# Modulation chunks moved out of the setup stage of a two-block transformer kernel, and semaphores cleared by range

## The reference, cut to what matters

```
c_act = silu(c)
for l in range(2):
    mod = c_act @ w_ada[l] + b_ada[l]              # w_ada[l]: 1024 x 6144
    shift1, scale1, gate1, shift2, scale2, gate2 = split(mod, 6)
    h = rms_norm(x, norm1_g[l]) * (1 + scale1) + shift1
    x = x + gate1 * mix(h)                         # attention and convolution
    h2 = rms_norm(x, norm2_g[l]) * (1 + scale2) + shift2
    x = x + gate2 * expert_choice_ffn(h2, ...)     # router, softmax, top_k, experts
```

## Time and profile before

| | us |
|---|---|
| median of the runs shown (3) | 3978.43 |
| their range | 3977.78 to 3983.3 |
| the profiled execution | 3975.68 |
| its span | 3973.9 |

### The profile page before, as it was taken

One profiled execution on the slowest core, in us unless ns is written; L12 is line 12 of the kernel. 1 busy time (PEld: TensorE's weight loads), 2 busy tenths in 40 slices (PEclk: granted clock), 3 DMA queues, 4 the chain that ended last, 5 costly groups with the idle time before them and its releaser, 6 DMA issues. The chain is left out here.

```text
span 3973.9 us, 47220 instructions
## 1 busy us (share of the span) xinstructions
PE 3517.1 (89%) x16392; PEld 2800.9 (70%) x16392; DVE 2466.7 (62%) x2229; ACT 1648.8 (41%) x1644; POOL 1170.1 (29%) x688
## 2 busy tenths in 40 slices
PE   4798798779999969879949999969998789999998
PEld 1375597558888757378728888857877678888886
DVE  7787775478888769777358888865118431212124
ACT  5521443258888630244227888843115110000101
POOL 0142233311111124133321111104542535453632
PEclk9899899889999979989969999989998889999999
DMA  9610001469999720000049999952100211111111
GB/s 339 242 38 18 10 14 38 164 242 395 395 395 396 299 77 32 14 15 20 32 186 358 394 393 395 394 203 95 48 29 0 85 38 58 53 42 53 43 52 53
DMA packets 143147, 610.67 MB, mean 154 GB/s; under 512 B 16480, under 2 KB 34272, under 8 KB 93920
## 3 DMA queue, kind: packets, MB, share of 16 engines
q1 hardware_dynamic: 133856, 576.21, 37.7%
q0 software_dynamic: 9216, 33.56, 3.3%
HBM read 563.06 MB, written 41.94 MB: 152 GB/s over the span
## 5 line engine op out<-in xcount | busy, mean ns | idle before, releaser
L1630 DVE TENSOR_TENSOR ex_lo<-ex_raw,ex_hi 128x2048 fp32r<-128x2048 f32 x378 | 858.5, 2291 | 115.6 <-ACT ex_hi L1580 115.0
L1580 ACT CAST ex_hi<-ex_raw 128x2048 fp32r<-128x2048 f32 x378 | 720.7, 1914 | 139.6 <-PE psum L1542 139.6
L1540 PE MATMUL psum<-ex_hi,xe_hi 128*128 128x512 f32 x1024 | 404.1, 395 | 1.3 <-DVE xe_lo L1635 1.3
L1542 PE MATMUL psum<-ex_hi,xe_lo 128*128 128x512 f32 x1024 | 400.7, 391 | 0.0
L1541 PE MATMUL psum<-ex_lo,xe_hi 128*128 128x512 f32 x1024 | 400.3, 391 | 0.0
L516 DVE SCALAR_TENSOR_TENSOR mix<-y,lcols,mix 128x1024 f32<-128x1024 f32 x176 | 278.8, 1585 | 5.7
L2399 DVE TENSOR_TENSOR ff_full<-psum,ff_full 128x1024 f32<-128x1024 f32 x22 | 26.9, 1225 | 408.4 <-PE psum L431 408.4
L416 POOL TENSOR_SCALAR up_hi<-up_raw 128x1024 fp32r<-128x1024 f32 x44 | 122.1, 2776 | 361.6 <-PE psum L431 337.6
L431 PE MATMUL psum<-hn_hi,up_hi 128*128 128x512 f32 x704 | 218.2, 391 | 5.3 <-DVE hn_lo L1753 5.2
L1540 PEld LDWEIGHTS psum<-ex_hi,xe_hi 128*128 128x128 f32 x1024 | 193.4, 189 | 40.9 <-issue 2.1
L1542 PEld LDWEIGHTS psum<-ex_hi,xe_lo 128*128 128x128 f32 x1024 | 193.2, 189 | 40.7
(11 more groups left out here) (404 smaller groups left out, 7748.6 us busy)
## 6 DMA issues: line engine op xcount, KB each, us to landing
ex_raw<-w_experts_dram SPq DMA_DIRECT2D x384, 1024.0 KB, 7.6
ada_w<-w_ada_dram SPq DMA_DIRECT2D x24, 2048.0 KB, 11.6
up_raw<-w_gate_up_dram SPq DMA_DIRECT2D x44, 512.0 KB, 3.3
in_raw<-w_in_dram SPq DMA_DIRECT2D x24, 512.0 KB, 3.4
p_raw<-w_in_dram SPq DMA_DIRECT2D x24, 512.0 KB, 3.4
wd_raw<-w_down_dram SPq DMA_DIRECT2D x11, 1024.0 KB, 5.4
lo_raw<-w_out_dram SPq DMA_DIRECT2D x16, 512.0 KB, 3.3
moe_rows<-zero_row SPq DMA_DIRECT2D x16, 512.0 KB, 4.5
```

Source lines behind the costliest of these rows:

```text
L1540: pe.matmul(bank(out), x_hi, h[:, k, :], start=first, stop=False)
L1542: mm = pe.matmul(bank(out), x_lo, h[:, k, :], start=False, stop=end)
L1580: act.copy(hi[j % PARTS][:], raw[j % RAW][:]).then_inc(w_hi, 1)
L1630: dve.tensor_tensor(lo[j % PARTS][:], raw[j % RAW][:], hi[j % PARTS][:].bitcast(F32), ALU.subtract).then_inc(w_lo, 1)
```

## The change

Setup computes the 8 chunks of `SETUP_CHUNKS`: (0, 0) to (0, 4) and (1, 2) to (1, 4), in 4 groups, from an array `w_ada_first` in which each partition's part of a tile is one run of 16 KB. The other four are computed as columns in float32, without split parts: a tile of 128 output channels (1024 x 128, 512 KB, from `w_ada_late`) is the stationary operand in 8 products, `c_act` the moving one. (l, 5) and (l + 1, 0) are computed in `route`, two tiles behind each of the 8 blocks of row transposes, from a ring of 3 buffers; (l + 1, 1) by 8 tiles behind the last expert, from expert weight buffers that have come free. Layer 1 counts l + 1 as 0 and computes those two again, unused. The transposes now read `rt_h` without POOL's copy, and the loops over blocks on SP and PE are written out. The clears are done for each range of consecutive numbers. `mod`, `b_ada` and `c_act` live until the second block.

```diff
+EARLY_MOD = 5
+SETUP_CHUNKS = [(0, n) for n in range(EARLY_MOD)] + [(l, n) for l in range(1, DEPTH) for n in range(2, EARLY_MOD)]
+ADA_GROUPS = len(SETUP_CHUNKS) * D // (HALF * ADA_BUFS)
+ADA_RING = 3
+ADA_LATE = 4
...
-                            if name not in before:
-                                pool.sem_clear(sem_names[name])
+                        first = 0
+                        for at in range(1, len(own) + 1):
+                            if at == len(own) or own[at] != own[at - 1] + 1:
+                                pool.sem_clear(range(own[first], own[at - 1] + 1))
+                                first = at
...
-                                sp.dma_start(ada_w[b][:], A["w_ada"][bass.ds(ADA_BUFS * i + b, 1)].rearrange(
-                                    "c (k p) n -> p (c k) n", p=P)).then_inc(ada_in[b], 16)
+                                sp.dma_start(ada_w[b][:], A["w_ada_first"][bass.ds(ADA_BUFS * i + b, 1)].rearrange(
+                                    "c p (k n) -> p (c k) n", n=HALF)).then_inc(ada_in[b], 16)
...
+                        dve.tensor_tensor(mod[:, 0, :], psum[:, 7, 0:first], b_ada[:, 0, 0:first], ALU.add).then_inc(added, 1)
+                        for later in range(1, DEPTH):
...
+        def mod_tile(pe, col, w, ready):
+
+            for k in range(DT):
+                mm = pe.matmul(col, w[:, k, :], c_act[:, k:k + 1], start=k == 0, stop=k == DT - 1)
+            mm.then_inc(ready, 1)
...
+                        for n in range(ADA_RING):
+                            load_ada(n)
                         for j in range(SPLIT_EARLY):
                             load_ahead(sp, 0, j, pieces)
-                        with sp.Fori(0, TB // 2) as i:
...
+                        for t in range(TB):
+                            sp.wait_ge(row_copied[t % 2], t // 2 + 2)
+                            sp.dma_start(h2_rows[t * P:(t + 1) * P, :], rows[:, t % 2, :]).then_inc(rows_out, 16)
+                            for n in range(2 * t, 2 * t + 2):
+                                if n + ADA_RING < 2 * DT:
+                                    sp.wait_ge(ada_used, n + 1)
+                                    load_ada(n + ADA_RING)
...
-                                pool.wait_ge(row_turned[b], i + 1)
-                                pool.tensor_copy(part[:, b, :, :], h[:, :, bass.ds((2 * i + b) * P, P)]).then_inc(part_in[b], 1)
...
                         dve.tensor_copy(slots[:], token).then_inc(slots_done, 1)
+                        dve.wait_ge(ada_used, 2 * DT)
+                        dve.tensor_tensor(gate, mod_psum[:, 0:DT], b_ada[:, bass.ds(l, 1), EARLY_MOD * DT:N_MOD * DT].rearrange(
...
+                        dve.tensor_tensor(mod[:, bass.ds(nxt, 1), 0:DT].rearrange("p l n -> p (l n)"), mod_psum[:, DT:2 * DT],
...
+                        for blk in range(TB):
+                            b = blk % 2
+                            pe.wait_ge(row_copied[b], blk // 2 + 1)
+                            for k in range(DT):
+                                mm = pe.transpose(banks(2 + 4 * b)[:, k * P:(k + 1) * P], h[:, k, blk * P:(blk + 1) * P], ident)
+                            mm.then_inc(row_turned[b], 1)
+                            for n in range(2 * blk, 2 * blk + 2):
+                                pe.wait_ge(ada_in[n % ADA_RING], 16 * (n // ADA_RING + 1))
+                                mod_tile(pe, mod_psum[:, n:n + 1], ada[n % ADA_RING], ada_used)
                         pe.wait_ge(place_done, 1)
...
+                        for n in range(ADA_LATE):
+                            sp.wait_ge(w_lo, PIECES * last + PIECES - RAW + n + 1)
+                            tiles = A["w_ada_late"][bass.ds(nxt * N_MOD * DT + DT + 2 * n, 2)]
...
                         expert(last, False)
+                        for n in range(ADA_LATE):
+                            pe.wait_ge(late_in[n], 16)
+                            for c in range(2):
+                                mod_tile(pe, psum[:, 0, 2 * n + c:2 * n + c + 1], late[n][:, c * DT:(c + 1) * DT, :], late_used)
...
                         expert(last, False)
+                        dve.wait_ge(late_used, 2 * ADA_LATE)
+                        dve.tensor_tensor(mod[:, bass.ds(nxt, 1), DT:2 * DT].rearrange("p l n -> p (l n)"), psum[:, 0, 0:DT],
```

More of the change, by code:

```diff
@@ L143, in _ @@
                     def _(pool):
-                        for name in sem_names:
-                            if name in ("ex_gathered", "ex_scattered") and name not in before:
+                        own = sorted(sem_names[name].num for name in sem_names if name not in before)
+                        for name in ("ex_gathered", "ex_scattered"):
+                            if name in sem_names and name not in before:
                                 pool.dma_reset(range(sem_names[name].num, sem_names[name].num + 1))
-                            if name not in before:
-                                pool.sem_clear(sem_names[name])
+                        first = 0
[3 more added lines that the diff above has]
+                                first = at
             sem_home[0] = home
@@ L166, in build @@
         x = sb("x", [P, DT, S])
-        mod = sb("mod", [P, DEPTH, N_MOD * DT])
         scols = sb("scols", [P, N_SC])
@@ L338, in _ @@
                         dve.wait_ge(rows_turned, 1 + ADA_GROUPS)
-                        dve.tensor_tensor(mod[:].rearrange("p l n -> p (l n)"), psum[:, 7, 0:DEPTH * N_MOD * DT], b_ada[:],
-                                          ALU.add).then_inc(added, 1)
+                        first = EARLY_MOD * DT
+                        dve.tensor_tensor(mod[:, 0, :], psum[:, 7, 0:first], b_ada[:, 0, 0:first], ALU.add).then_inc(added, 1)
+                        for later in range(1, DEPTH):
+                            at = first + (later - 1) * (EARLY_MOD - 2) * DT
+                            dve.tensor_tensor(mod[:, later, 2 * DT:first], psum[:, 7, at:at + first - 2 * DT],
+                                              b_ada[:, later, 2 * DT:first], ALU.add).then_inc(added, 1)
         def spread(pe, out, diag, ready):
@@ L1252, in experts_part @@
                     pieces = (expert_pieces(l), raw, hi, lo, loaded, w_hi, w_lo)
-                    route(l, gain, shift, slots, slot_gate, pieces)
-                    run_experts(slots, slot_gate, pieces)
+                    route(l, gain, shift, gate, slots, slot_gate, pieces)
+                    run_experts(l, slots, slot_gate, pieces)
                 combine(gate)
@@ L1264, in load_ahead, with route @@
             load_piece(sp, raw[j % RAW], e + ahead // PIECES, ahead % PIECES).then_inc(loaded[j % RAW], 16)
-        def route(l, gain, shift, slots, slot_gate, pieces):
+        def mod_tile(pe, col, w, ready):
+            for k in range(DT):
+                mm = pe.matmul(col, w[:, k, :], c_act[:, k:k + 1], start=k == 0, stop=k == DT - 1)
+            mm.then_inc(ready, 1)
+        def route(l, gain, shift, gate, slots, slot_gate, pieces):
             load_piece, raw, hi, lo, loaded, w_hi, w_lo = pieces
@@ L1287, in route @@
                 pick = sb("rt_pick", [P, 3, EXPERTS], F32, ctx)
-                part = sb("rt_part", [P, 2, DT, P], F32, ctx)
+                ada = [sb(f"rt_ada{i}", [P, DT, P], F32, ctx) for i in range(ADA_RING)]
+                ada_in = [sem(f"rt_ada_in{i}") for i in range(ADA_RING)]
+                ada_used, mods_done = sem("rt_ada_used"), sem("rt_mods_done")
+                nxt = (l + 1) % DEPTH
+                mod_psum = psum[:, 1, 0:2 * DT]
                 names = ("w_in", "scaled", "h_ready", "logits", "logit_copied", "turned", "soft", "exp_done", "aff_done",
@@ L1306, in _, with load_ada @@
                             load_piece(sp, raw[j], 0, j).then_inc(loaded[j], 16)
+                        def load_ada(n):
+                            at = l * N_MOD * DT + EARLY_MOD * DT + n if n < DT else nxt * N_MOD * DT + n - DT
+                            sp.dma_start(ada[n % ADA_RING][:], A["w_ada_late"][bass.ds(at, 1)].rearrange(
+                                "c p (k m) -> p (c k) m", m=P)).then_inc(ada_in[n % ADA_RING], 16)
+                        for n in range(ADA_RING):
+                            load_ada(n)
                         for j in range(SPLIT_EARLY):
                             load_ahead(sp, 0, j, pieces)
[L1309 to L1312 removed]
+                        for t in range(TB):
[5 more added lines that the diff above has]
+                                    load_ada(n + ADA_RING)
                         sp.wait_ge(zeroed, 16 * TB)
@@ L1440, in expert_pieces, with run_experts @@
             return load
-        def run_experts(slots, slot_gate, pieces):
+        def run_experts(l, slots, slot_gate, pieces):
             _, raw, hi, lo, loaded, w_hi, w_lo = pieces
@@ L1464, in run_experts @@
                 last = EXPERTS - 1
+                nxt = (l + 1) % DEPTH
```

(10 more changed lines are left out.)

28 lines of the change are left out of this document (11 added, 17 removed).

## The result

| | us |
|---|---|
| before, median of 6 runs | 3978.41 (3977.78 to 3983.3) |
| after, median of 6 runs | 3997.49 (3993.46 to 4003.87) |
| ratio after/before | 1.0047, 95% interval 1.0034 to 1.006 |
| the profiled execution after | 4003.87, its span 4002.1 |

The change makes the kernel about 19 us (0.5%) slower. The forecast was 4000 on the profiled execution and 4002 on the median.

The account below looks back on a forecast made before the run. Bounds: DVE in setup and routing, POOL's clears at stage ends, the scatter at the experts' end. On 3975.68: -44.8 + 0.2 - 21.6 + 0.8 + 64.6 + 24.4 = +23.6, 3999.3; forecast 4000, range 3955 to 4020.

Parts of the forecast that it names:

- The clock in routing: Routing's 256 one-column passes run at TensorE's low clock throughout, so the loop outlasts DVE's search: +32.3 us a layer.
- The experts' end: 128 more passes behind the last expert, the clock falling after 4.3 us: combine starts 12.2 us later a layer.
- Setup: Two of six groups go at 22.39 us each, -44.8 us; the final addition becomes two, +0.2.
- Loads in 16 KB runs: Setup's weight loads in longer runs: no gain, as nothing waits for a load; a loss excluded.
- Clears: Stage ends: seven range clears replace 325 single ones, 318 x 0.068 = 21.6 us gained, all on the path.
- gap of 0.8 us at the mixing stage's end: Sign of being right: with range clears the gap there is 0.8 instead of 6.8 us.
- The small terms: Two additions at DVE's end in routing, before the gather: +0.4 us a layer; the ring's loads add nothing.
- The high clock: Rival: all passes at the high clock, routing delay 0, experts' end 3.4 us a layer; 3917 us, 12%.
- the mixed one: Rival: about half the routing loop's passes at high clock, delay about 16 there, 8 at experts' end; 3958 us, 8%.
- The costly range clear: Rival: a range clear costs as much as its members, so the clears gain nothing; 4021 us, 8%.
- the upper edge of the forecast: The forecast's slow end, 4011 us: routing 33.5 and experts' end 16.3 us a layer; the forecast had 72%.

Follow-up runs that it names:

- wide: The changed kernel with each added product's moving column streamed 128 times, only the first result column used; 3931.74 us, ratio to before 0.9877.
- runs_16k: The kernel before with only the memory layout of setup's weights changed, to 16 KB runs; one execution, 3974.09 us.
- clears_only: The kernel before with only the semaphore clears done by range; 3958.38 us, ratio to before 0.9946.

## Why the prediction was right, step by step

Each of the four parts did what was forecast of it, and the measured median lies 4.5 us below the forecast's 4002. Two sizes explain most of that: over both layers the routing term was 6.1 us too large and the experts' end 2.1 too small. That the profiled execution came so near to 4000 is partly such variation, as said below the landmarks.

**The clock in routing**, the crux, held: 256 passes, 0.50 throughout. The term was +32.3 us a layer and measured +29.4 (-51.1 to -21.7) and +29.1 (-13.8 to +15.3). It was sized a little large: I took 3.45 us for 16 passes, and in a long run they pitch at 6.69 / 32 = 0.209, 3.35 for 16; the transposes took 1.74, not 1.8. Together that is 2.2 of the 3 us a layer. The Trainium skill, "TensorE: Matmul & The Clock Gate", section "LDWEIGHTS (loading the stationary operand)", gives P / 1.2 ns for P columns, with no term for the clock. The trace agrees at the high level, where the pitch of a pass is 0.112 us (wide, 3.57 / 32), and not at the low one, where it is 0.209.

**The experts' end**: +12.2 a layer forecast; from `ye` to combine's first memset 11.53 us became 24.71, +13.2, and +13.3 in layer 1. The clock fell as I said, behind the end of the dense work, but earlier: 0.90 over 1360 to 1366 means high until 1364.8, 3.4 us after 1361.37, where I had taken 4.3 from the earlier trace rows. So some nine passes more ran at the low price, about 1 us.

**Setup**: -44.6 forecast, -46.4 measured. The two groups came out to the tenth. The other 1.7 us is the start of setup, which varies by up to 2 us between executions in either layout (runs_16k); that it fell on the good side here is luck. "Loads in 16 KB runs: no gain, as nothing waits for a load" leaves out that DVE's first wait, ahead of the groups, is for a load, the small input `scols`. For the weights it is true, and no run shows that the 16 KB runs gain or lose any time.

**Clears**: -21.6 forecast; 7 instructions, as counted, and -21.5 measured alone (interval -15 to -28). The trace's own gaps give somewhat less, 5.6 at each mixing end, 4.2 at layer 0's experts' end and 1.0 at setup's, as the long ranges are not single clears of 38 ns. The prediction's gap of 0.8 us at the mixing stage's end became 1.23.

**The small terms**: from `place_f`'s transpose to the gather's first copy it is 3.56 us (800.05 less 796.49) and was 3.13: +0.4, as said. No load made PE wait in the full change, in either layer.

**The rivals.** The high clock (3917) is out by the windows, and so is the mixed one (3958): not one block of the loop ran fast. `wide` shows that the high level can be had in this loop, with the same passes made wide. The costly range clear (4021) is out by clears_only. One sum of the prediction is off by 1: the upper edge of the forecast, by its own terms, is 4010 and not 4011.

## What to carry to other kernels

A product with one moving column cost as much here as one with 128: at the high level 16 passes last 1.84 to 1.94 us with one column and 1.95 with 128. A run of the narrow ones left PE 100% busy at half clock for 67 us; with the column streamed 128 times the same loop ran at full clock from its second block on. So before filling an engine's idle time with such work, price it at the low clock, and compare that with the idle time that the stage really has: the loop had 37 us of room, and the work was 67 us at the low level and 42 with all but the first block at the high one.
What ends a stage is worth reading instruction by instruction: 318 clears fewer, at a pitch of 68 ns, gained 21 us by themselves, while the 44.6 us won by moving two groups out of setup were more than lost where the work went.

## What the runs showed that I had not expected

- More streamed columns made the loop shorter: 67.5 us with 1 column, 42.3 with 128, the weights and passes being equal.
- With fast passes the ring's loads (three buffers of 512 KB) come onto the path: in `wide`, layer 0, PE waits for five of the sixteen tiles, 3.1 us together (0.2 to 1.1 each), and turns `place_f` 4.8 us after DVE has it ready (766.39). A deeper ring wasn't tried. Without these waits the loop would still be some 39 us, an estimate from 42.3 less 3.1.
- A range clear's time grows with its length: 139 ns for 19 semaphores, 526 for 91, that is about 5.4 ns for each further one.
- Run length counts for the rate of transfers in flight together, though not for this kernel's time. From 5 to 30 us the queues moved 382 and 383 GB/s in the two kernels with 2 KB runs (before, clears_only) and 406 to 411 in the seven with 16 KB runs. The Trainium skill, "DMA: Bandwidth & Descriptors", section "Specifications", gives 512 bytes as the least transfer for line rate; the trace doesn't agree, as 2 KB runs were 6% slower than 16 KB ones.

The window of the kernel before, then that of runs_16k:

```profile
5.00:30.00 25.00, 0.00 (x0) 0.00 (x0) 15.11 (x20) 5.18 (x10) 0.00 (x0) 1.00 0.99 382
```

```profile
5.00:30.00 25.00, 0.00 (x0) 0.00 (x0) 16.15 (x21) 6.73 (x11) 0.00 (x0) 1.00 1.00 407
```
